# A chunked recurrence on one core: triangular products at half width, copies moved between engines, another order of steps

## The reference, cut to what matters

```python
def step(S, inp):
    rt, wt, kt, vt, at, bt = inp
    S = (S * wt[:, :, None, :] + jnp.einsum('bhvk,bhk->bhv', S, at)[..., None] * bt[:, :, None, :]
         + vt[..., None] * kt[:, :, None, :])
    return S, jnp.einsum('bhvk,bhk->bhv', S, rt)
```

## Time and profile before

| | us |
|---|---|
| median of 3 runs | 3277.62 (3275.03 to 3281.9) |
| profiled execution, own time | 3286.38 |
| its span in the trace | 3284.2 |
| PE busy | 3041.3 (93%) |
| DVE busy | 1586.4 (48%) |
| POOL busy | 1384.1 (42%) |
| ACT busy | 930.9 (28%) |

### The profile page before, as it was taken

The page is one execution under the profiler, slowest core; times in us unless marked ns, Lnnn a source line. Parts: engine busy times, 40 slices in busy tenths (PEclk is TensorE's granted clock), DMA queues, the critical chain, the costliest instruction groups (busy, mean ns, idle before and its releaser), DMA issues.

```text
span 3284.2 us, 74630 instructions
## 1 busy us (share of the span) xinstructions
PE 3041.3 (93%) x32844; PEld 2848.5 (87%) x32844; DVE 1586.4 (48%) x2107; ACT 930.9 (28%) x1560; POOL 1384.1 (42%) x1047
## 2 busy tenths in 40 slices
PE   7999988989999999979999788888878999999997
PEld 6989856979999999969999776776668999999996
DVE  5032264138666631254122355777623776664125
ACT  4132265232111111134111255555433311111111
POOL 2323320226777743512433333444433477774320
PEclk8999998899999999989999889999989999999998
DMA  3353443221233343213322222212052222323311
GB/s 99 122 133 111 153 160 114 80 96 59 80 83 116 84 140 120 53 64 142 124 90 92 76 63 76 71 53 70 21 187 77 78 78 78 110 78 136 136 42 62
DMA packets 342475, 312.31 MB, mean 95 GB/s; under 512 B 35335, under 2 KB 303059, under 8 KB 341020
## 3 DMA queue, kind: packets, MB, share of 16 engines
q1 hardware_dynamic: 325706, 275.99, 27.7%
q10 hardware_dynamic: 16466, 31.83, 2.6%
HBM read 212.79 MB, written 94.62 MB: 94 GB/s over the span
## 4 chain that ended last, share of the span: by engine, by line
PE 40%; DVE 6%; issue 4%; ACT 1%; SPq 1%; DMA 1%; POOL 1%; ACTq 0%; DVEq 0%; POOLq 0%
PE PS L521 17%; PE PS L688 12%; PE PS L2814 2%; PE PS L2820 1%; PE PS L2826 1%; PE PS L2804 1%; PE PS L2808 1%; PE PS L702 1%; DVE act_lo L2516 1%; PE PS L2800 1%; SPq L496 0%; PE PS L2961 0%; DMA rw<-z_st 0%; PE PS L708 0%; DVE g_AK L3272 0%
## 5 line engine op out<-in xcount | busy, mean ns | idle before, releaser
L521 PE MATMUL PS<-act_hi,w_hi 128*128 128x344 f32 x1992 | 641.1, 322 | 38.0 <-DVE act_lo L2150 22.0
L521 PE MATMUL PS<-act_lo,w_hi 128*128 128x344 f32 x1992 | 637.7, 320 | 0.0
L521 PE MATMUL PS<-act_hi,w_lo 128*128 128x344 f32 x1992 | 637.2, 320 | 0.0
L502 POOL CAST w_hi<-w_raw 128x1024 fp32r<-128x1024 f32 (+1 forms) x119 | 127.3, 1070 | 1086.3 <-PE PS L521 559.2
L521 PEld LDWEIGHTS PS<-act_hi,w_hi 128*128 128x128 f32 x1992 | 376.3, 189 | 43.6 <-issue 29.3
L521 PEld LDWEIGHTS PS<-act_hi,w_lo 128*128 128x128 f32 x1992 | 376.3, 189 | 0.0
L521 PEld LDWEIGHTS PS<-act_lo,w_hi 128*128 128x128 f32 x1992 | 376.3, 189 | 0.0
L688 PE MATMUL PS<-T,wq_S 128*128 128x258 f32 x2880 | 365.7, 283 | 0.0
L688 PE MATMUL PS<-act_hi,wq_A 128*128 128x258 f32 x1920 | 364.5, 282 | 0.0
L688 PEld LDWEIGHTS PS<-T,wq_S 128*128 128x128 f32 x2880 | 354.4, 189 | 0.0
L688 PEld LDWEIGHTS PS<-act_hi,wq_A 128*128 128x128 f32 x1920 | 305.4, 190 | 0.0
(11 more groups left out here) (609 smaller groups left out, 6014.6 us busy)
## 6 DMA issues: line engine op xcount, KB each, us to landing
hidd<-hid_out SPq DMA_DIRECT2D x44, 516.0 KB, 3.3
w_raw<-in_ffn_w_gate_dram SPq DMA_DIRECT2D x44, 512.0 KB, 4.8
w_raw<-in_ffn_w_up_dram SPq DMA_DIRECT2D x44, 512.0 KB, 6.1
w_raw<-in_ffn_w_down_dram SPq DMA_DIRECT2D x32, 512.0 KB, 3.7
hid_in<-hidd SPq DMA_DIRECT2D x28, 516.0 KB, 7.3
proj<-stage ACTq DMA_DIRECT2D x24, 516.0 KB, 2.7
xT<-xkeep SPq DMA_DIRECT2D x3, 4128.0 KB, 17.8
rw<-z_st SPq DMA_DIRECT2D x24, 516.0 KB, 2.8
```

Source lines behind the costliest of these rows:

```text
L502: nc.gpsimd.tensor_copy(w_hi[:, u, 0:kts, :], w_raw[:, u, 0:kts, :]).then_inc(w_hi_done, 1)
L521: mm = nc.tensor.matmul(PS[:, 3 * u + c, 0:CH], w[:, u, kt, :], x[:, kt, CH * c:CH * c + CH], start=(kt == 0 and part == 0), stop=(kt == k ...
```

## The change: what it does

1. Triangular products. `pX64` now forms for each head one product of input half 0 for output half 0 (64x64) and one with all 128 input rows for output half 1 (128x64). Both go to bank 6 + e, where e is the head's place in its pair. The fourth product for i_T64 stays. `pAS` has 8 products, each with all 128 output columns. `pU` has two products for each head, into bank 6 alone, with i_X11 for the first output half and i_XC (128 rows, the off-diagonal block above the diagonal one) for the second. The products of zeros are gone, and so are ACT's copies `rhs7` and `u7`; DVE copies instead of adding.
2. GpSimd's `diag` and `xad` become copies on ACT: `xd` (four of 32x256 elements) and `xa` (two). m_pair is gone. GpSimd clears i_X11, i_XC and i_Xa once.
3. Another order on every engine; among others `R` moves one item earlier, and the loads of item k+4 now wait for `b` of item k+2 rather than `R`.

```diff
-        i_XD, i_X21, i_Xa, i_T64 = (room(f"i_{n}", [P, GH, DH]) for n in ("XD", "X21", "Xa", "T64"))
+        i_X11, i_XC, i_Xa, i_T64 = (room(f"i_{n}", [P, GH, DH]) for n in ("X11", "XC", "Xa", "T64"))
...
-        BG = Order(sem("sc_pool"), "rkm:i b:s sum:o diag:i xad:i kp:p R:s rk:p o:o", AHEAD, -3, ITEMS + 1, ITEMS)
+        BG = Order(sem("sc_pool"), "rkm:i b:s kp:p sum:o o:o rk:p R:p", AHEAD, -3, ITEMS + 1, ITEMS)
...
-                        sp.wait_ge(BG.sem, BG.of("R", n - 2))
+                        sp.wait_ge(BG.sem, BG.of("b", n - 2))
...
-                    tt(blocks(i_XD), spread(i, 1), in_pairs, ALU.mult).then_inc(BG.sem, BG.turn("diag", i))
...
-                    tt(blocks(i_Xa), spread(i, 0), in_pairs, ALU.mult).then_inc(BG.sem, BG.turn("xad", i))
...
-                    mm(PS[half(0), 7, 0:GP * DH], nothing, S[half(1), :, :].rearrange("p q v -> p (q v)"), start=True, stop=False, skip_group_check=True)
-                    for h in range(GH):
-                        V = [t_V[half(a), n % 3, P * (h % GP) + DH * (h // GP):P * (h % GP) + DH * (h // GP) + DH] for a in range(2)]
-                        for a, b in ((0, 0), (1, 1), (0, 1)):
-                            mm(part(h, a, b), g_AK[half(a), n % 2, h, half(b)], V[a], start=(h == 0), stop=False, skip_group_check=True)
-                        ins = mm(PS[half(0), 3, DH * h:DH * h + DH], i_T64[half(1), h, :], i_XD[half(1), h, :], start=True, stop=True)
+                    pe.wait_ge(BA.sem, BA.of("xd", n))
+                    for q in range(GP):
+                        for e in range(2):
+                            h, col, v = GP * e + q, slice(DH * q, DH * q + DH), slice(P * q + DH * e, P * q + DH * e + DH)
+                            mm(PS[half(0), 6 + e, col], g_AK[half(0), n % 2, h, half(0)], t_V[half(0), n % 3, v], start=(q == 0), stop=False, skip_group_check=True)
+                            mm(PS[half(1), 6 + e, col], g_AK[:, n % 2, h, half(1)], t_V[:, n % 3, v], start=(q == 0), stop=False, skip_group_check=True)
+                            ins = mm(PS[half(0), 3, DH * h:DH * h + DH], i_T64[half(1), h, :], i_XC[half(1), h, :], start=True, stop=True)
                     ins.then_inc(BP.sem, BP.turn("pX64", n))
                     for q in range(GP):
-                        for e, b in ((0, 0), (1, 1), (0, 1), (1, 0)):
-                            ins = mm(part(GP * e + q, e, b), f_A[half(e), n % 2, q, half(b)], S[half(e), q, :], start=False, stop=True, skip_group_check=True)
+                        for e in range(2):
+                            ins = mm(PS[:, 6 + e, DH * q:DH * q + DH], f_A[half(e), n % 2, q, :], state(n)[half(e), q, :], start=False, stop=True, skip_group_check=True)
...
-                    mm(PS[half(0), 7, :], nothing, flat(q_rhs)[half(1), :], start=True, stop=True, skip_group_check=True)
-                    for h in range(GH):
-                        rhs = [q_rhs[half(a), h // GP, h % GP, :] for a in range(2)]
-                        mm(part(h, 0, 0), i_XD[half(0), h, :], rhs[0], start=(h == 0), stop=True, skip_group_check=True)
-                        mm(part(h, 1, 1), i_XD[half(1), h, :], rhs[1], start=(h == 0), stop=True, skip_group_check=True)
-                        ins = mm(part(h, 0, 1), i_X21[half(0), h, :], rhs[0], start=(h == 0), stop=True, skip_group_check=True)
+                    for e in range(2):
+                        for q in range(GP):
+                            h = GP * e + q
+                            mm(PS[half(0), 6, DH * h:DH * h + DH], i_X11[half(0), h, :], q_rhs[half(0), e, q, :], start=True, stop=True)
+                            ins = mm(PS[half(1), 6, DH * h:DH * h + DH], i_XC[:, h, :], q_rhs[:, e, q, :], start=True, stop=True)
...
+                    for b in range(4):
+                        ins = nc.scalar.copy((i_X11, i_XC)[b // 2][quad(b), :, quad(b % 2)], i_X[quad(b), n % 2, 1, :, :])
+                    ins.then_inc(BA.sem, BA.turn("xd", n))
...
-                    nc.scalar.copy(flat(q_rhs), PS[:, 7, :]).then_inc(BA.sem, BA.turn("rhs7", n))
...
-                    nc.scalar.copy(flat(q_u), PS[:, 7, :]).then_inc(BA.sem, BA.turn("u7", n))
...
-                    tt(flat(q_rhs), PS[:, 6, :], flat(q_rhs), ALU.add).then_inc(BV.sem, BV.turn("rhs", n))
...
+                    nc.vector.tensor_copy(q_rhs[:, :, :, :].rearrange("p e q v -> p e (q v)"), PS[:, 6:8, 0:DH * GP]).then_inc(BV.sem, BV.turn("rhs", n))
```

More of the change, by code:

```diff
@@ L2827, in level_X @@
                 return ins
-            part = lambda h, a, b: PS[half(b), 6 + a, DH * h:DH * h + DH]
             state = lambda j: q_S[:, j % NG, (j // NG) % 2, :, :]
-            nothing = m_incl[half(1), 0:DH]
             pe.wait_ge(VM.sem, len(VM.names) + START)
@@ L2951, in scan_tensor @@
                     turn(f_in["v"][:, s % 2, :, :]).then_inc(BP.sem, BP.turn("ptV", s))
+                if live_n:
+                    pe.wait_ge(BA.sem, BA.of("tK", n))
+                    pe.wait_ge(BV.sem, BV.of("rhs", n))
+                    for q in range(GP):
+                        for e in range(2):
+                            col = slice(P * q + DH * e, P * q + DH * e + DH)
+                            mm(PS[half(e), 7, DH * q:DH * q + DH], t_K[:, n % 2, col], t_V[:, n % 3, col], start=(q == 0), stop=False, skip_group_check=True)
                 if live_i:
@@ L2980, in scan_tensor @@
                 if live_s:
+                    pe.wait_ge(BV.sem, BV.of("A", s))
                     pe.wait_ge(BV.sem, BV.of("B", s))
-                    pe.wait_ge(BA.sem, BA.of("tV", s))
-                    turn(f_B).then_inc(BP.sem, BP.turn("ptB", s))
+                    if s:
+                        pe.wait_ge(BA.sem, BA.of("rkc", s - 1))
+                    scores(0, f_B, f_A[:, s % 2, :, :]).then_inc(BP.sem, BP.turn("pN", s))
+                if live_i:
+                    pe.wait_ge(BA.sem, BA.of("t16", i))
+                    level_X(i).then_inc(BP.sem, BP.turn("pX16", i))
+                if live_n:
+                    for q in range(GP):
+                        for e in range(2):
+                            mm(PS[half(e), 5, P * q:P * q + P], state(n)[half(e), q, :], f_R[half(e), n % 3, q, :], start=False, stop=False, skip_group_check=True)
                 if live_i:
@@ L3002, in scan_tensor @@
                     ins.then_inc(BP.sem, BP.turn("pX32", i))
-                if live_n:
-                    pe.wait_ge(BV.sem, BV.of("u", n))
-                    pe.wait_ge(BV.sem, BV.of("rb", n))
-                    for q in range(GP):
-                        for e in range(2):
-                            ins = mm(PS[half(e), 5, P * q:P * q + P], q_u[:, e, q, :], g_RB[:, n % 2, GP * e + q, :], start=False, stop=True, skip_group_check=True)
-                    ins.then_inc(BP.sem, BP.turn("pY", n))
             pe.wait_ge(BV.sem, BV.of("S", ITEMS - 1))
@@ L3042, in scan_scalar @@
                     act.wait_ge(BP.sem, BP.of("pX32", n))
-                    act.wait_ge(BG.sem, BG.of("xad", n))
+                    if n:
+                        act.wait_ge(BP.sem, BP.of("pT64", n - 1))
                     nc.scalar.copy(i_Xa[quad(1), :, quad(0)], PS[quad(1), 3, 0:32 * GH].rearrange("p (h t) -> p h t", t=32)).then_inc(BA.sem, BA.turn("w21", n))
+                    act.wait_ge(BV.sem, BV.of("xs16", n))
+                    if n:
+                        act.wait_ge(BP.sem, BP.of("pT64", n - 1))
+                    for b in range(2):
+                        ins = nc.scalar.copy(i_Xa[quad(b), :, quad(b)], i_X[quad(b), n % 2, 0, :, :])
+                    ins.then_inc(BA.sem, BA.turn("xa", n))
                 if live_i:
@@ L3049, in scan_scalar @@
                     act.wait_ge(BP.sem, BP.of("pX32", n))
-                    act.wait_ge(BG.sem, BG.of("diag", n))
+                    if n:
+                        act.wait_ge(BP.sem, BP.of("pU", n - 1))
                     for b in (0, 2):
-                        ins = nc.scalar.copy(i_XD[quad(b), :, quad(1)], PS[quad(b), 3, 32 * GH:64 * GH].rearrange("p (h t) -> p h t", t=32))
+                        ins = nc.scalar.copy((i_X11, i_XC)[b // 2][quad(b), :, quad(1)], PS[quad(b), 3, 32 * GH:64 * GH].rearrange("p (h t) -> p h t", t=32))
                     ins.then_inc(BA.sem, BA.turn("x21", n))
+                    act.wait_ge(BP.sem, BP.of("pT64", n))
+                    nc.scalar.copy(wide(i_T64[half(1), :, :]), PS[half(1), 2, :]).then_inc(BA.sem, BA.turn("t64", n))
                 if live_s:
@@ L3324, in scan_vector @@
                     add_X(4, i)
+                    turn_X(4, i)
                 if live_s:
```

243 lines of the change are left out of this document (107 added, 136 removed).

## The result

| | before | after |
|---|---|---|
| median, 4 runs each on one chip, us | 3276.32 (3273.56 to 3281.9) | 3339.17 (3329.12 to 3346.49) |
| profiled execution, us | 3286.38 | 3329.12 |

The changed kernel is slower by 62.9 us; the ratio is 1.0188, 95% interval 1.0157 to 1.0218. The forecast was 3346 us. So the two traces can explain 2.8 us an iteration, while the medians say 3.9 (62.9 / 16).

The account below looks back on a forecast made before the run. TensorE was taken as the bound (busy 93% of the span). Terms 4.6 - 0.5 + 0.3 - 0.15 = +4.25 us an iteration, times 16 = +68 us, gave 3346 us from 3277.6, range 3254 to 3368.

Parts of the forecast that it names:

- The first term: Products of `pX64`, `pAS`, `pU` on TensorE: about 0.145 us at each change of shape, +4.6 us an iteration.
- free overlap: Rival: 64-row and 128-row products run side by side in different columns; -1.05 us an iteration, 3261 us; chance 0.27.
- no gap: Rival: shapes don't overlap, but changing costs no gap; +1.85 us an iteration, 3307 us; chance 0.15.
- i_T64: ScalarE's copy now ahead of f_t, so TensorE's wait before `pX64` goes: -0.5 us an iteration.
- `xa`: With `xd`, new ScalarE copies before `pT64` that may delay TensorE: +0.3 us an iteration, bounds 0 to 0.8.
- The loads: Start after `b`, earlier in the iteration; gaps inside TensorE's groups move, no change counted; -1.4 us if they halved.
- GpSimd and VectorE: GpSimd loses `diag` and `xad`, VectorE copies instead of adding: 0 for both, GpSimd's from 0 to -0.1 us.
- fewer instructions: 104 fewer of some 2000 TensorE instructions an iteration; gaps inside groups shrink 5% of 2.8 us, -0.15 us.
- the new order: Swaps such as `pBU` ahead of `pN` hide hardly any waits: 0, from -0.3 to +0.3 us.
- The loads decide: Rival: moved loads cut gaps and low clock, -22 us; 3324, or 3239 with free overlap; the latter case's chance 0.04.
- ScalarE becomes late: Rival: `xd` and `xa` cost 0.8 rather than 0.3 us an iteration, adding 8 us; no chance of its own given.
- one pair: Two TensorE gaps 126 entries (252 instructions) apart, read as the instruction stream arriving in blocks.

Follow-up runs that it names:

- the kernel with one shape: Changed kernel with its 128-row products cut to the lower 64 rows in `pX64` and `pU`, so all are 64 by 64: 3250.28 us, ratio 0.9925 to before.
- the isolated edit: Kernel before, with only ScalarE's copy of i_T64 moved ahead of the four f_t: 3269.02 us, ratio 0.9975 to before.
- the sorted kernel: Changed kernel with the same products of `pX64` and `pU` sorted by shape (64 or 128 rows): 3253.02 us, ratio 0.9939 to before.
- the kernel with the loads held back: The sorted kernel, with the loads of item k+4 moved from `b` of item k+2 to `R` of item k+3: 3249.41 us, ratio 0.9910 to before.

## Why the prediction was right, and which terms were off

**The first term had the right mechanism.** Each change of shape has its price, and it goes when the changes are taken out (33 stretches to 4, and `pU`'s 16 to 2 alone). The distance over a change, read as 0.145 us from boundaries between groups, is 0.15 in `pX64`. But that this number is so near the 0.146 that a stretch more costs is chance: in `pU` the prediction's steps make a change dearer than a step within a shape by 0.145 - 0.061 = 0.084 us, and (4.11 - 2.14) / 14 = 0.141 was measured. The missing part is the slow step behind a change, which comes next. The rivals "free overlap" (3261) and "no gap" (3307) fall with it: L2865 to L2867 would have taken 1 and 2.9 us, and they take 4.4.

**It was mis-sized by 1.4 us an iteration:** 9.56 us of products against 8.1 (+6.0, not +4.6).
- `pU` 4.11, not 3.3. The second entry behind a change starts 0.11 us after the first (0.33 for a pair, less 0.22 for one), not 0.061. The 0.061 is a mean over 16 entries of one shape, and a mean hides that its first step is the slow one, as the kernel with one shape shows (0.10, then 0.06). With 2 entries a stretch that step is the only one: 8 x 2 x 0.05 = 0.8.
- `pX64` 4.41, not 4.0. The head was right within 0.02 us (0.52 against 0.50) because two errors cancelled: 0.05 more in the 128-row pair, and the products of two heads side by side where I had set them one behind the other. The outermost stretches make up the rest.
- `pAS` 1.04, not 0.8. It goes like L2814, whose weights have 128 columns, not like L2978. Both had been named as ends; I chose the middle.

**What held.** i_T64: the wait ahead of `pX64` is gone, and the isolated edit gave 7 us, where 0.5 x 16 = 8 was counted. `xa`: the wait ahead of L2835 is about 0.3 us where it occurs, as forecast, but it comes only every other iteration, 1.7 us in 11.6, so the term was 0.15. The loads: their burst moved (see the stretches below), and moving them again changed nothing that is shown. GpSimd and VectorE: nothing.

```profile
2182.00:2184.00 2.00, 2.00 (x110) 1.80 (x97) 0.61 (x1) 0.86 (x2) 0.46 (x1) 1.00 0.93 244
...
2196.00:2198.00 2.00, 1.81 (x93) 1.50 (x83) 1.58 (x4) 1.97 (x5) 0.00 (x0) 1.00 1.12 313
```

These are stretches of 2 us of after. The transfers of an item now come in two bursts, with `pU` between them, where before one burst met the dense stretch.

**What failed: "fewer instructions", -0.15 us.** I let the gaps shrink in proportion to the instructions, by 5%. They fell from 3.7 to 1.6 us an iteration, -2.1. About 0.8 of that came with the new order (2.9 with the old products in it), for which I had counted no change. The rest came with the products, and the runs say that their count isn't what matters. With one count of 32012 matmuls, the gaps in 415 us are 18.5 with mixed products, 14.9 with sorted ones and 36.7 with one shape; with 32844, 46.8, and 38.4 in the new order. Beside the time that `pX64`, `pAS` and `pU` take together, all in the new order, the gaps an iteration are 2.9 us with the old products (3.5 us), 2.7 with one shape (3.2 to 3.8), 2.5 with only `pU` new (4.1), 1.1 sorted (5.3) and 1.6 mixed (9.6). So they shrink when these steps get slower, as if the supply of instructions caught up meanwhile, but not further beyond 5 us. The step was off by (2.1 - 0.15) x 16 = 31 us over the loop.

**The sum again:** +6.0 (products) - 2.1 (gaps) - 0.4 (other waits, 10.6 to 5.5 us in the window) = +3.5 an iteration, 56 us over 16, against 62.9 measured. That the forecast of +4.25 came near, 3346 us against 3339, is luck in part: an underestimate of 1.4 and an overlooked gain of 2.1 largely offset each other. The range of 3254 to 3368 us also took in both rivals on the products, so it decided nothing; the timeline and the sorted kernels did. In the two traces the iteration grew by 2.8 only; the mean granted clock rose from 0.96 to 0.98, which is 0.7 us of 35.7 and would close the difference, but no run isolates it.

**Rivals.** "The loads decide" finds no support in the kernel with the loads held back. Nor do the gaps need busy transfers, as the prediction had it: that of 1.13 us ahead of 2139.3 in before falls where they move 0 GB/s. "ScalarE becomes late" cost no more than forecast. The rival that I didn't have is a floor in the supply of instructions: four kernels with quite different products (sorted; sorted with late loads; one shape; old `pX64` with sorted `pU`) end at 3249 to 3253 us. The transfers of instructions have a queue of their own, 1930 to 2345 us (packets, MB, share of 16 engines). In the trace of before:

```profile
q8 instruction: 94, 1.54, 1.5%
```

In that of after:

```profile
q8 instruction: 81, 1.33, 1.4%
```

That is 16.4 KB a packet, in before 7.4 of them an iteration. TensorE has 11956 matmul entries in this window before and 10318 after, so 127 of them go with each packet in both. The gaps lie on the same grid. Between one "issue" gap of before and the next stand 126, 255, 126, 378, 127, 127, 128, 253 entries and so on to the end of the window: each of the 46 distances is a whole multiple of about 127, and so are those of after and of the kernel with one shape. With its weight load each entry is two instructions, so a gap falls only where a block of some 254 of them ends, as the prediction had guessed from one pair. About half of the blocks before have one (47 gaps, 94 packets), and after about a quarter (22, 81). The page "Runtime: NRT & Kernel Launch" of the Trainium skill, Instruction fetch mechanics, calls the cost of crossing a block "mostly hidden". Here the gaps at such crossings hold 46.8 of 415 us. That the instructions are late there is still inferred; no run moved the supply itself. And it isn't a floor of one fixed rate: the kernel with the old products in the new order has 12428 entries in the same 415 us where that with one shape has 11880, and it is as fast as the sorted kernel (0.9939 both) with 832 matmul entries more in the program. What holds these kernels near 3250 us stays open.

## What to carry to other kernels

Sort small matmuls by the shape of their weights (rows x columns of the array) before counting them: here 29 changes of shape in an iteration cost 68 us of TensorE's time over the loop and 81 us in the program, for the same products. Ahead of such an edit, look for the two or three records just behind a change, not for the mean of a long group. And where an engine has gaps that nothing releases, a saving in its busy time may come back as gaps. One run that leaves work out measures how far it does. To tell where such gaps come from, count the entries between them: an even spacing across different steps speaks for the instruction stream.
